# A hybrid decoder block on one core: most of the down projection by seven quarter products instead of eight

## The reference, cut to what matters

```python
def conv_ffn(h, w_up, conv_w, conv_b, w_down):
    u = h @ w_up                                  # (2048, 1024) @ (1024, 5632)
    u = conv(u, width 3, causal, per channel) + conv_b
    gate, val = jnp.split(u, 2, axis=-1)          # 2816 columns each
    return (jax.nn.gelu(gate, approximate=True) * val) @ w_down   # (2048, 2816) @ (2816, 1024)
```

## Time and profile before

| | us |
|---|---|
| median of three runs | 2240.99 |
| profiled execution, device time | 2238.74 |
| its span, first to last instruction | 2237.0 |
| PE busy | 2199.5 |
| DVE busy | 1211.8 |
| ACT busy | 749.2 |
| POOL busy, all of it in block one | 228.1 |

### The profile page before, as it was taken

How to read it: one execution, slowest core, us unless ns; L and a number is a source line. 1 busy time by engine, 2 the same in 40 slices (tenths; PEclk the granted TensorE clock), 3 DMA queues, 4 the chain that set the end, 5 groups by cost and what they waited for, 6 DMA issues and landing times.

```text
span 2237.0 us, 35236 instructions
## 1 busy us (share of the span) xinstructions
PE 2199.5 (98%) x13099; PEld 1775.2 (79%) x13099; DVE 1211.8 (54%) x2154; ACT 749.2 (33%) x1521; POOL 228.1 (10%) x150
## 2 busy tenths in 40 slices
PE   7999999999999999999999999999999999999998
PEld 4776788888887778888888778888888877888886
DVE  3577683857767564252555845244355665515244
ACT  3555533343445331111235542122024444212012
POOL 2322344444200000000000000000000000000000
PEclk9999999999999999999999999999999999999999
DMA  9964689877663446555564345655546344555553
GB/s 373 401 232 184 231 314 325 289 287 282 238 233 115 177 181 228 198 193 188 184 229 152 142 150 208 234 188 194 198 163 240 131 168 150 207 193 200 190 189 149
DMA packets 114430, 476.86 MB, mean 213 GB/s; under 512 B 7935, under 2 KB 38921, under 8 KB 69257
## 3 DMA queue, kind: packets, MB, share of 16 engines
q1 hardware_dynamic: 114313, 475.24, 58.1%
HBM read 372.45 MB, written 102.76 MB: 212 GB/s over the span
## 4 chain that ended last, share of the span: by engine, by line
PE 93%; ACT 3%; DVE 2%; DMA 1%; issue 1%; SPq 0%; POOL 0%; DVEq 0%; ACTq 0%; POOLq 0%
PE ps L614 18%; PE ps L616 18%; PE ps L615 17%; PE ps L639 9%; PE ps L641 9%; PE ps L640 9%; PE ps L1026 1%; PE ps L1029 1%; PE ps L1027 1%; PE ps L716 1%; PE ps L566 1%; PE ps L763 1%; ACT XN L1170 1%; DMA raw<-in_w_in_dram 1%; PE ps L884 1%
## 5 line engine op out<-in xcount | busy, mean ns | idle before, releaser
L614 PE MATMUL ps<-hTh,wt 128*128 128x512 f32 x1792 | 708.1, 395 | 2.3 <-DVE hTl L1566 2.0
L616 PE MATMUL ps<-hTh,wt 128*128 128x512 f32 x1792 | 698.7, 390 | 0.0
L615 PE MATMUL ps<-hTl,wt 128*128 128x512 f32 x1792 | 698.7, 390 | 0.0
L614 PEld LDWEIGHTS ps<-hTh,wt 128*128 128x128 f32 x1792 | 336.7, 188 | 80.3 <-issue 11.3
L616 PEld LDWEIGHTS ps<-hTh,wt 128*128 128x128 f32 x1792 | 336.8, 188 | 71.3
L615 PEld LDWEIGHTS ps<-hTl,wt 128*128 128x128 f32 x1792 | 337.0, 188 | 67.0
L1883 DVE TENSOR_SCALAR cv<-ub,CW 128x512 f32<-128x512 f32 x176 | 101.1, 575 | 464.8 <-ACT ub L1426 450.7
L1426 ACT ACTIVATE ub<-ps 128x512 f32<-128x512 f32 x176 | 105.1, 597 | 682.7 <-PE ps L616 632.9
L639 PE MATMUL ps<-wt,pTh 128*128 128x512 f32 x692 | 270.3, 391 | 0.0
L641 PE MATMUL ps<-wt,pTh 128*128 128x512 f32 x692 | 269.4, 389 | 0.0
L640 PE MATMUL ps<-wt,pTl 128*128 128x512 f32 x692 | 269.4, 389 | 0.0
(11 more groups left out here) (280 smaller groups left out, 2355.9 us busy)
## 6 DMA issues: line engine op xcount, KB each, us to landing
wt<-split_w SPq DMA_DIRECT2D x264, 1024.0 KB, 4.8
split_w<-wt SPq DMA_DIRECT2D x88, 1024.0 KB, 7.0
raw<-in_w_up_dram SPq DMA_DIRECT2D x22, 1024.0 KB, 9.9
XT<-in_w_ada_dram SPq DMA_DIRECT2D x10, 1024.0 KB, 11.9
XN<-in_x_dram SPq DMA_DIRECT2D x4, 2048.0 KB, 9.5
raw<-in_w_in_dram SPq DMA_DIRECT2D x8, 1024.0 KB, 14.9
XR<-in_x_dram SPq DMA_DIRECT2D x4, 2048.0 KB, 10.3
raw<-in_w_down_dram SPq DMA_DIRECT2D x8, 1024.0 KB, 9.2
```

Source lines behind the costliest of these rows:

```text
L614: mm(ps[:, bank, :], w, hTh[:, k, :], start=(k == 0), stop=False)
L615: mm(ps[:, bank, :], w, hTl[:, k, :], start=False, stop=False)
L616: ins = mm(ps[:, bank, :], wl[:, slot, k, :], hTh[:, k, :], start=False, stop=(k == KD - 1))
```

## The change

The 22 hidden tiles are now made in five groups: four of two up steps (4 tiles) and one of three (6 tiles, called LG). The down product of a group of 4 is one product of (512 tokens x 512 hidden) by (512 hidden x 1024), cut into quarters and done with seven quarter products (Strassen's scheme in Winograd's form). A quarter product, q0 to q6, is one unit of 12 matmuls: 2 token tiles by 2 slices by 3. The last group is done as before. So:

- DVE makes four sums and differences of the hidden quarters per up step (`token_half_sums`), and the high and low parts cover seven quarters of 256 tokens (two instructions, 768 and 1024 wide) instead of two tiles of 512.
- The weights' four sums and differences per group are made once, in block one, by POOL (`differ`) in the freed `XN` and `T32`, and split and kept like any unit.
- The down product of group f stands after the first two up units of group f+1, on PE, ACT and DVE.
- Its PSUM banks (4 to 7, and 2 and 3) are drained after each quarter product, as the next adds on top of them: 14 additions to `Y` by DVE per group, of which the first group gives 8 to ACT as copies.
- In blocks two to four the weights have six slots (two in the place of `raw`).
- The loops of the MLP are written out.
- The next block's norm moves from the second down product to the steps of LG.

```diff
+NS = (2, 2, 2, 2, 3)
+LEFT = (0, 2, 3, 4, 6, 5, 1)
+BANK = (4, 6, 2, 4, 2, 4, 4)
+RAW_OF = (0, 1, 4, 0, 3, 2, 1)
+COPIES, ADDS = (0, 2, 3, 6), (1, 4, 5)
+SLOTS = 6
...
 POOL
+            def differ(out_, a, c):
+                pool.tensor_tensor(quarter(out_), quarter(a), quarter(c), ALU.subtract).then_inc(s["t_added"], 1)
...
+            for n in range(RING, UNITS):
+                pool.wait_ge(s["unit_done"], n - RING + 1)
+                low(n)
+                if n in UP_OF and UP_OF[n][0] < LG and UP_OF[n][1:] == (1, 1):
...
+                    differ(4, 2, 0)
...
+                    differ(2, 3, 2)
+                if n in DN_OF and DN_OF[n][1] == 0:
...
+                    differ(0, 3, 4)
+                if n in DN_OF and DN_OF[n][1] == 3:
...
+                    differ(1, 1, 0)
 PE
+                def down_unit(f, q):
+                    n = DN_UNIT[f] + q
+                    weights(n)
+                    for t in range(2):
+                        if q < 2 and f == 0:
+                            pe.wait_ge(s["t32_ready"], tb + 12)
+                        elif q == 2:
+                            pe.wait_ge(s["acc_taken"], eb_ + (E_IN + 4 * (ST0[f] + 1) + 2 + t + 1))
+                        else:
+                            name, count = evac(b, *((f - 1, 6), (f - 1, 1), None, (f, 0), (f, 2), (f, 3), (f, 5))[q], t)
+                            pe.wait_ge(s[name], count)
+                        for k in range(2):
+                            pe.wait_ge(s["p_ready"], b * (2 * STEPS) + (2 * (ST0[f] + k) + (1 if LEFT[q] < 3 else 2)))
...
+                for f in range(1, NF):
+                    up_units(f, 0, (0, 1))
+                    for q in range(7):
+                        down_unit(f - 1, q)
+                    up_units(f, 0, (2, 3))
+                    for i in range(1, NS[f]):
+                        up_units(f, i, range(4))
+                last_down()
 ACT, in up_step
                     take_up(0)
                     take_up(1)
+                    if f and i == 0:
+                        down(f - 1)
+                    if f == LG and i == 1 and not last:
+                        next_squares()
                     take_up(2)
                     gelu(0)
                     take_up(3)
                     gelu(1)
...
+                    act.wait_ge(s["prod_ready"], jb + 2)
+                    act.activation(flat(pTh[:, i, 0:3, :]), flat(P32[:, 1:4, :]), ACT.Copy).then_inc(s["ph_ready"], 1)
+                    act.wait_ge(s["sums_ready"], b * ST0[LG] + (st_ + 1))
+                    act.activation(flat(pTh[:, i, 3:7, :]), flat(P32[:, 4:8, :]), ACT.Copy).then_inc(s["ph_ready"], 1)
 DVE
+                def down(f):
+                    for q in range(7):
+                        for t in range(0 if f == 0 and q in COPIES else 2):
...
+                            tt(y, y, ps[:, BANK[q] + t, :], ALU.add).then_inc(s["y_added"], 1)
...
+                    def token_half_sums():
...
+                        up(tt(s1, a21, a22, ALU.add))
+                        up(tt(s3, a11, a21, ALU.subtract))
+                        up(tt(s2, s1, a11, ALU.subtract))
+                        tt(s4, a12, s2, ALU.subtract).then_inc(s["sums_ready"], 1)
...
+                    conv(0)
+                    conv(1)
+                    if f and i == 0:
+                        down(f - 1)
...
+                    conv(2)
+                    gated(0)
+                    conv(3)
+                    gated(1)
+                    if f < LG:
+                        token_half_sums()
+                    hidden_low(0)
+                    hidden_low(1)
 SP, blocks two to four
+                def refill(n):
+                    sp.wait_ge(s["unit_done"], ub_ + (n - SLOTS + 1))
+                    fetch(b, n)
```

More of the change, by code:

```diff
@@ new lines, with sequence @@
+LEFT = (0, 2, 3, 4, 6, 5, 1)
+BANK = (4, 6, 2, 4, 2, 4, 4)
+DEST = ((2, 0), (2, 0), (0, 1), (2, 1), (2, 1), (0, 1), (0, 0))
+RAW_OF = (0, 1, 4, 0, 3, 2, 1)
+T_TURN = {2: 1, 5: 2, 3: 3, 6: 4}
+COPIES, ADDS = (0, 2, 3, 6), (1, 4, 5)
+Y_SUMS = 2 * len(ADDS) + (LG - 1) * 14
+Y_ADDS = Y_SUMS + 8
+FINAL = {(2, 0): 1, (2, 1): 4, (0, 1): 5, (0, 0): 6}
+DN_K = ((0, 1), (2,), (3, 4), (5,))
+def sequence():
+    up, down, n = {}, {}, U_IN + U_OUT
+    for f in range(NF):
+        for i in range(NS[f]):
+            for u in range(4):
+                up[f, i, u], n = n, n + 1
+                if f and i == 0 and u == 1:
+                    down[f - 1] = n
+                    n += 7
+    down[LG] = n
+    return up, down, n + 8
@@ new lines, with pair_of, width @@
+UP_UNIT, DN_UNIT, UNITS = sequence()
+assert UNITS % RING == 0
+UP_OF = {n: key for key, n in UP_UNIT.items()}
+DN_OF = {DN_UNIT[f] + q: (f, q) for f in range(LG) for q in range(7)}
+def pair_of(n):
+    if n in UP_OF:
+        f, i, u = UP_OF[n]
+        return (U_IN + U_OUT) // 2 + 2 * (ST0[f] + i) + u // 2, u % 2
+    if n >= DN_UNIT[LG]:
+        v = n - DN_UNIT[LG]
+        return (U_IN + U_OUT) // 2 + 2 * STEPS + v // 2, v % 2
+    return n // 2, n % 2
+def width(n):
+    return 512 * len(DN_K[(n - DN_UNIT[LG]) % 4]) if n >= DN_UNIT[LG] else 1024
@@ L57 @@
[L57 removed]
+EVACS = E_IN + 4 * STEPS
 G_BANKS = (4, 7, 4, 7)
@@ L419, in first_block @@
                 load_x(0)
[L420 to L437, removed]
+                def load_up(k):
+                    col = (k // 2) * 256 + (k % 2) * FF
+                    load((OFF_OUT + U_OUT + 2 * k) // 2 % 2, w_up_d[:, :, col:col + 256], KD)
@@ L438, in first_block @@
+                for n in range(SLOTS):
+                    if n < 2:
+                        sp.wait_ge(s["w_lo"], UNITS)
+                    else:
+                        sp.wait_ge(s["unit_done"], UNITS + n - SLOTS + 1)
+                        sp.wait_ge(s[f"kept{n - 2}"], 4 * UNITS)
+                    fetch(1, n)
                 store_out(0)
@@ L1044, in one_block, with hidden, last_down @@
+                def hidden(k, t):
+                    return tuple(y[:].rearrange("p i j n -> p (i j n)")[:, k * BT + t * P:k * BT + t * P + P] for y in (pTh, pTl))
+                def last_down():
+                    late = 1 if first else 0
+                    for u in range(8):
+                        i, n = u % 4, DN_UNIT[LG] + u
+                        if not last and u in (0, 1 + late, 2 + late):
                             if u == 0:
                                 pe.wait_ge(s["xn_ready"], b * 8 + 12)
-                                pe.wait_ge(s["y_added"], b * 16 + 16)
+                                pe.wait_ge(s["y_added"], b * Y_ADDS + Y_SUMS)
@@ L1483, in one_block @@
+                for u in range(4):
+                    if u:
+                        refill(DN_UNIT[LG] + u + RING)
+                    for k in (range(4), (4, 5), (6, 7), ())[u] if not last else ():
+                        prep(0, k)
+                        if k == 1:
+                            refill(DN_UNIT[LG] + RING)
+                sums_ = b * Y_ADDS + Y_SUMS
                 if last:
                     for t in range(TT):
-                        act.wait_ge(s["y_added"], b * 16 + (8 + 8 + t + 1))
+                        act.wait_ge(s["y_added"], sums_ + t + 1)
@@ L1933, in one_block @@
+                for f in range(NF):
+                    for i in range(NS[f]):
+                        up_step(f, i)
+                assert up.n == UP_STEPS, up.n
+                last_down()
                 if last:
```

581 lines of the change are left out of this document (317 added, 264 removed).

## The result

| | us |
|---|---|
| before, median of four runs | 2240.66 (2240.00 to 2242.86) |
| after, median of four runs | 2381.55 (2379.53 to 2383.10) |
| ratio after / before | 1.0626, interval 1.0608 to 1.0645 |
| forecast, its range | 2263, 2216 to 2294 |

The changed kernel is 6.3% slower, 140.9 us. Slower was forecast, with 22 us; the time lies far outside the range.

What follows compares the result with a forecast made beforehand. PE was taken to bound the MLP everywhere, with DVE, slowed by POOL, hardly behind it in block one. 2238.74 - 43.5 (matmuls) + 43.5 + 15.4 (block one's waits) + 9 (clock) = 2263 us, range 2216 to 2294.

Steps and rivals of the forecast that it cites:

- The saving on PE: All blocks: 192 matmuls fewer, 43.5 us saved on PE, 10.9 of them in block one and 32.6 in the others.
- The MLP of the later blocks is hidden: Blocks two to four: DVE's sums, parts and additions and the weight fetches fit behind PE's own work, so PE never waits.
- I take nothing for all of this: Blocks two to four: no cost for DVE's late steps, additions and the next block's norm; bounds 0 to 3 us.
- Block one, the waits: Block one's MLP: PE waits for DVE at quarter products, 15.4 us in group one and 14.5 in each of three others.
- The price of 2.05 us per POOL instruction: Block one's MLP: each POOL instruction takes 2.05 us from DVE; gain and loss balance at about 1.5.
- Block one, the clock: Block one: PE's clock falls after long waits, 2.2 us each, counted for four waits, 9 us.
- The tail is free: Rival, block one: DVE's two convolutions escape POOL's low parts, only q0 is late, 19 us; about 2214 us; chance 15%.
- DMA sets block one: Rival, block one: DMA traffic of 352 GB/s frees slots late on top of the sum, 2290 to 2310 us; chance 7%.
- Slow fetches: Rival, blocks two to four: weight fetches too slow for the quarter products, 18 us on top, 2281 us; chance 3%.
- Everything hidden: Rival, block one: nothing is late and the whole saving shows, 2195 to 2200 us; chance 8%.
- Waits in the later blocks: Sign of a wrong forecast: PE waits in blocks two to four, where none were expected in the MLP.

Runs made afterwards that it cites:

- e1: The changed kernel with ACT's combined logarithm and exponential table loaded in every block again, not in block four alone: 2293.17 us, 1.0231 of before.
- e4: e1 with POOL's low parts and differences in block one's MLP cut to 256 of 1024 columns (output not the reference's): 2195.4 us, one run.
- e2: The kernel before the change, with the combined logarithm and exponential table loaded in block four only: 2329.26 us, 1.0393 of before.
- e3: e1 with DVE's additions of the previous group's down product ahead of the next step's first two convolutions: 2254.57 us, 1.0062 of before.

## Why the prediction was wrong, point by point

**The saving on PE: right.** -10.6 us in after's last MLP, -11.3, -9.9 and -10.8 in e1, against -10.9 per block.

**The MLP of the later blocks is hidden: right.** PE is busy for 335.00 of 335.00 us in after's window of block two. The parts measured 0.951 and 1.226 us and a sum of 256 0.425, against 0.95, 1.22 and 0.42 estimated. No wait on a fetch appears.

**"I take nothing for all of this", and no term at all for the mixer of blocks two to four: this is the step that failed.** The passage has 0 to 3 us as bounds, the mixer isn't in it, and the two together cost 88.4 us (e1), 29.5 per block. It took DVE, PE and the fetches into account, and of ACT only the next norm's instructions, at 1.2 us each; the table that they need was never looked at. The trace of before had the row of 1.283 us per load, 15 times. The changed kernel has a load ahead of the logarithm and the exponential of each norm of blocks two to four. Neither was used. Without these 88.4 us the measured time is e1's 2293.2, just inside the range (2216 to 2294), but by its width alone: block one too came out 28 us dearer than forecast.

**Block one, the waits: in the right places, and 7% small in sum, partly by luck.** Forecast: q0 late by 9.5 in group one and 3.2 in the others, q6 of group one 5.9, q3 of the others 11.3; 58.9 us. Measured in after: 6.84, then 4.65, 7.08 and 7.69; 7.81, then 9.69, 9.26 and 10.14; 63.2 us. Errors of both signs cancel in it. q0 was too cheap in groups two to four. In group one a wait of 3.03 us for issue (at 295.63) stands ahead of the 6.84, and the two together are near the 9.5. q3's wait ends 19.5 us after q0's in each of groups two to four, where the forecast had the bank free after 19.4; the wait is shorter than 11.3 because PE comes late to it, with a fallen clock. q6's wait in group one ends 26.08 us after q0's, where 22.2 were forecast: DVE met eight POOL instructions there, not six. The price of 2.05 us per POOL instruction came out as 2.03, and e4 shows that without POOL's length nothing else holds PE up.

The Trainium skill, SBUF — State Buffer, section SBUF: two separate sides, calls the ports that DVE and GpSimd share an exclusive lock, which the loser waits out whole. The 128 x 2 copies of 2.38 and 2.25 us (0.16 and 0.17 with POOL idle) agree with it, and so do the additions from PSUM that lose nothing.

**Block one, the clock: mis-sized.** e1's block one is 85.0 us longer than before's. With the saving of 10.9 that is 95.9 to be explained. The windows from the first MLP to the second, before and then e1:

```profile
247.91:788.54 540.63, 538.20 (x3201) 438.55 (x3201) 367.57 (x526) 223.86 (x416) 158.36 (x66) 1.00 0.69 249
248.55:874.22 625.67, 552.21 (x3153) 445.96 (x3153) 474.10 (x598) 242.34 (x428) 233.01 (x94) 0.93 0.66 244
```

PE's idle time grew from 2.4 to 73.5 us, by 71: 63.9 at the quarter products, 4.5 at the next block's scaling, 2.8 of issue. The other 25 us are in its busy time, 552.2 us for matmuls that take 538.2 - 10.9 = 527.3 at the clock of before: that is the clock, where 9 stood in the forecast. It is 2.5 us for each of the ten waits; the forecast had 2.2, but for four waits. It left out those at q0, since another wait follows close by. The clock did fall behind q0 and come back to 1.00 (325.00 to 335.30) before the next wait, but what PE loses there isn't a cost of its own, since the next wait ends when DVE is ready, and is shorter by as much. So waits and clock have to be taken together: 95.9 us, where 67.9 were forecast. The two small waits, at the scaling and issue, were not foreseen.

**The sum.** Forecast 2263. Plus 5 for the quarter products' waits, 7 for the small waits and 16 for the clock: 2291, against 2292.4 of e1's profiled run. Plus 87.1 for the tables, the difference of the two profiled runs: 2378, against 2379.5 of after's. The terms are taken from the same runs, so this shows that nothing large is left out, and no more.

**The rivals.** *The tail is free* fell: all six POOL instructions of the tail met the convolutions in groups two and three, and eight in group one. *DMA sets block one* fell: 344 GB/s with PE full in e4. *Slow fetches* fell. *Everything hidden*, given 8%, is what e4 shows to be there for a shorter POOL, at 2195.4 (forecast 2195 to 2200). None of the rivals was about ACT's tables. "Waits in the later blocks" stood among the signs of a wrong forecast, and that sign came.

What stays open: why e2 has waits of 7.4 us on a fetch that e1 and after don't have, why q0 was later than forecast in groups two to four, and what ended the 2.8 us wait for issue in block one.

## What to carry to other kernels

When loops are rewritten, look at each condition whose variables changed their scope, and count the instructions of both programs by kind before pricing any: 15 table loads that become over a hundred are worth more than the whole saving. An engine with room to spare is no evidence that its part of the list costs nothing; here a chain of short dependent instructions ahead of a block's MLP set the time, with ACT busy for 38% of the span. Beside GpSimd, put what reads PSUM first and what goes from SBUF to SBUF last (38.6 us in e3), and count VectorE's price there by meetings as well as by work.

## What the runs showed of the hardware

- A table load lasted 1.283 us at every line that had one, and the next `ACTIVATE` starts 0.01 to 0.02 us behind it: in the rows of after, the pair of logarithm and exponential takes 2.58 us more than in those of before, two loads and no more. A logarithm and an exponential behind it took two loads, at each norm of blocks two to four, and none in e1, where the set that has both was loaded by name. The Trainium skill, ScalarE: Activation LUTs, section What ACT_TABLE_LOAD costs, gives 1283 ns for the load, which agrees, and about 1380 ns for a drain with it, which this trace doesn't show. Its section Table sets: the hidden batching unit counts one load for a logarithm and then an exponential, since one set has both; at the norms of blocks two to four of after there were two per pair.
- Short waits cost clock each time: after a wait of 6.9 us the granted clock was 0.50 (the 1.2 GHz level) for 3.9 us and 0.86 over the next 4, and after another of 7.9 us, 18 us later, 0.63 over 3.8 us. PE was busy for 25 us longer over ten waits in e1's block one, some 2.5 us per wait.
- One core had 344 GB/s over 340 us in e4, with PE busy for all of it.
